# One kernel, one core: row vectors spread by products, weight chunks of 512 columns, and ten slots for gathered rows

## What is computed

```python
def first_block(...):
    for l in range(2):
        sh1, sc1, g1, sh2, sc2, g2 = split(silu(c) @ ada_w[l] + ada_b[l], 6)
        mix = hybrid_mixer(modulate(x, sh1, sc1), ...)
        x = layer_norm(ALPHA * x + (1 + g1) * mix, ln1_g[l], ln1_b[l])
        ffn = peer(modulate(x, sh2, sc2), ...)
        x = layer_norm(ALPHA * x + (1 + g2) * ffn, ln2_g[l], ln2_b[l])

def peer(h, ...):                       # 8 heads x 16 picks = 128 experts for each token
    u = u_tab[experts]                  # rows of 1024 float32
    act = gelu(sum(u * h)) * g
    return sum(act * v_tab[experts])
```

## Time and profile before

| | |
|---|---|
| time, median of 3 runs | 2900.17 us (2894.32 to 2902.61) |
| the profiled execution, its own time | 2893.22 us |
| its span, first to last instruction | 2891.4 us |
| PE, DVE, ACT, POOL busy | 1891.9, 1803.3, 374.6, 1071.4 us |
| mean granted clock of PE | 0.80 of full speed |
| DMA | 860.86 MB, mean 298 GB/s |
| gathers (software queue) / SP's loads | 538.12 MB / 321.24 MB |

### The profile page before, as it was taken

The page is one execution under the profiler, slowest core; times in us unless marked ns, Lnnn a source line. Parts: engine busy times, 40 slices in busy tenths (PEclk is TensorE's granted clock), DMA queues, the critical chain, the costliest instruction groups (busy, mean ns, idle before and its releaser), DMA issues.

```text
span 2891.4 us, 23615 instructions
## 1 busy us (share of the span) xinstructions
PE 1891.9 (65%) x8197; PEld 1332.9 (46%) x8197; DVE 1803.3 (62%) x3281; ACT 374.6 (13%) x830; POOL 1071.4 (37%) x1047
## 2 busy tenths in 40 slices
PE   7889444185644363454364467767188999988998
PEld 4668111064342151142251156643157786477873
DVE  1436999889678889979889986676944200142001
ACT  1311001022102010002011000000014100131000
POOL 1002444577355555755556765465600000000000
PEclk8989556586776685776678788889579999999999
DMA  8366999999999999999999999999860544512443
GB/s 288 111 217 226 399 399 401 369 376 374 371 402 404 400 401 391 336 368 399 399 403 374 339 348 392 368 405 405 323 237 30 189 150 156 189 61 90 157 146 116
DMA packets 359975, 860.86 MB, mean 298 GB/s; under 512 B 23721, under 2 KB 146865, under 8 KB 359729
## 3 DMA queue, kind: packets, MB, share of 16 engines
q0 software_dynamic: 148288, 538.12, 48.4%
q1 hardware_dynamic: 211568, 321.24, 31.9%
HBM read 858.23 MB, written 1.05 MB: 297 GB/s over the span
## 4 chain that ended last, share of the span: by engine, by line
PE 36%; DMA 33%; DVE 14%; issue 11%; POOL 3%; ACT 2%; SPq 0%; DVEq 0%; ACTq 0%
PE bank L927 13%; DMA RING<-in_peer_v,EX 10%; PE bank L415 8%; DMA W<-in_w_ada 6%; PE bank L941 5%; DMA W<-in_ada_w 4%; DMA RING<-in_peer_u,EX 3%; PE bank L424 3%; DMA WORK<-in_peer_u,EX 3%; DMA W<-in_w_up 2%; DVE ACC L1680 2%; POOL RING L1041 2%; PE bank L447 2%; DMA W<-in_w_gate 2%; DMA WORK<-in_peer_v,EX 2%
## 5 line engine op out<-in xcount | busy, mean ns | idle before, releaser
L927 PE MATMUL bank<-HT,W 128*128 128x256 f32 x2112 | 482.0, 392 | 61.6 <-DMA W<-in_w_up 30.3
L927 PEld LDWEIGHTS bank<-HT,W 128*128 128x128 f32 x2112 | 414.8, 197 | 128.6 <-DMA W<-in_w_up 33.9
L1041 POOL DMA_INDIRECT RING<-in_peer_u,EX x343 | 326.4, 952 | 378.8 <-DVE ACC L1662 244.7
L1662 DVE SCALAR_TENSOR_TENSOR ACC<-RING,hrows 128x1024 bf16<-128x1024 f32 x343 | 406.2, 1217 | 79.9 <-DMA RING<-in_peer_u,EX 77.6
L1041 POOL DMA_INDIRECT RING<-in_peer_v,EX x341 | 379.2, 1112 | 206.6 <-DVE hrows L1680 91.5
L447 PE MATMUL bank<-W,CACT 128*32 128x512 f32 x704 | 149.9, 955 | 237.5 <-DMA W<-in_w_ada 135.3
L403 PE MATMUL bank<-consts,XN 128*128 128x128 f32 x208 | 44.6, 397 | 312.4 <-DVE XN L1505 144.6
L415 PE MATMUL bank<-W,HT 128*128 128x256 f32 x992 | 228.7, 394 | 18.6 <-ACT HT L1101 7.4
L941 PE MATMUL bank<-W,WORK 128*128 128x512 f32 x528 | 229.3, 597 | 14.4 <-DVE WORK L2279 14.4
L1041 POOL DMA_INDIRECT WORK<-in_peer_v,EX x171 | 193.7, 1133 | 100.1 <-DVE hrows L1680 39.2
L2279 DVE TENSOR_TENSOR WORK<-WORK,bank 128x256 f32<-128x256 f32 x66 | 27.2, 420 | 321.3 <-ACT WORK L1401 321.3
(11 more groups left out here) (356 smaller groups left out, 2332.1 us busy)
## 6 DMA issues: line engine op xcount, KB each, us to landing
W<-in_w_ada SPq DMA_DIRECT2D x48, 1024.0 KB, 16.4
W<-in_ada_w SPq DMA_DIRECT2D x40, 1024.0 KB, 12.9
W<-in_w_gate SPq DMA_DIRECT2D x33, 1024.0 KB, 5.5
W<-in_w_up SPq DMA_DIRECT2D x33, 1024.0 KB, 5.6
W<-in_w_down SPq DMA_DIRECT2D x33, 1024.0 KB, 5.0
W<-in_w_in SPq DMA_DIRECT2D x32, 1024.0 KB, 13.6
W<-in_peer_wq SPq DMA_DIRECT2D x22, 1024.0 KB, 17.4
W<-in_w_out SPq DMA_DIRECT2D x12, 1024.0 KB, 5.3
```

The source lines that it names most:

```text
L927: mm = pe.matmul(bs[j][:, g * S:(g + 1) * S], w[:, k, j * P:(j + 1) * P], HT[:, k, :], start=(k == 0 and g == 0), stop=(k == DC - 1 and g ...
L1041: gp.indirect_dma_start(SLOT[g % NS], None, rows, bass.IndirectOffsetOnAxis(EX[:, t, k:k + 1], 0))\
L1662: ve.scalar_tensor_tensor(out=JUNK[:, g % 2, :], in0=SLOT[g % NS], scalar=1.0, in1=HB[:, :], op0=ALU.mult, op1=ALU.mult, accum_out=ACTS[:, ...
```

## The change

1. `ROWS` (8 KB of each partition) goes, `ROWM` (4 KB) comes: 20 vectors, one on each of 20 partitions, loaded once by POOL in ten small DMAs. A vector is spread by a product of a column of the identity, broadcast, with `ROWM` (`spread_into`): into a PSUM bank of its own (`spread`, two banks of 512 for a vector), or, for the biases of gates, added in the bank of the gate.
2. The 1 that is added to the gates of the first model comes from ACT's copy (bias `one`), and the DVE instructions that added bias and 1 go.
3. `layer_norm` of layer 0 and the last `scaled_rows` still have rows from loads: the first two by POOL at the start into `HN` and `ACC`, the last two by SP into `HN` and `GA[:, 3, :]`. Of 14 pairs of loaded rows two are left.
4. `NS = 10`; seven slots lie in `RING`.
5. In the feed-forward a chunk is 4 blocks of rows by 512 columns (rows of 2 KB), four banks are open at a time; the last two of 22 columns of blocks stay as they were.
6. The plan of `stage(0, 0, 1)` has eight steps of `c0` in place of nine, since `gate_rows` is one step; ACT no longer waits for `gated` within `ada` of `c0`.

```diff
-        NS = 9
+        NS = 10
-        ROWS = sb("ROWS", [P, 2, D])
+        ROWM = sb("ROWM", [P, D])
+            def spread_into(b, kind, l, hf, start):
+                r = ROW_AT[kind] + l
+                return pe.matmul(b[:, :], ident[0:NROWS, r:r + 1].to_broadcast([NROWS, P]), ROWM[0:NROWS, hf * 512:(hf + 1) * 512],
+                                 start=start, stop=True)
+            def spread(name, kind, l):
+                for hf in range(2):
+                    b = open_bank((*name, hf), "V")
+                    spread_into(b, kind, l, hf, True).then_inc(filled, 1)
...
                         pe.matmul(b[:, :], const("who")[:, who:who + 1].to_broadcast([P, P]), ROWT[:, half, :],
-                                  start=True, stop=True).then_inc(filled, 1)
+                                  start=True, stop=False)
+                        spread_into(b, ("ada_" if p[0] == "b" else "ada2_") + "12"[(q - 8) // 2], int(p[1]), q % 2, False)\
+                            .then_inc(filled, 1)
...
-                load_rows(d["ln1_g"][l], d["ln1_b"][l])
+                spread(("ln1", p, t, 0), "ln1_g", l)
+                spread(("ln1", p, t, 1), "ln1_b", l)
...
                 modulated(p, 2, 2, VA)
+                if who == "l":
+                    spread(("post", "l1", l), ("post_mix", "post_ffn")[l], 1)
-                for c in range(NF // 2):
+                for f0 in range(0, NF, 4):
+                    nf = min(4, NF - f0)
                     bs = []
                     for g, src in enumerate((wg, wu)):
+                        parts = 2 if nf == 4 else 1
+                        for kh in range(parts):
+                            ks = range(kh * DC // parts, (kh + 1) * DC // parts)
+                            w = weight(src[:, ks.start:ks.stop, f0 * P:(f0 + nf) * P])
+                            for j in range(nf):
+                                if g == 0 and kh == 0:
+                                    bs.append(open_bank(("gu", p, f0 + j), "V"))
+                                for k in ks:
+                                    mm = pe.matmul(bs[j][:, g * S:(g + 1) * S], w[:, k - ks.start, j * P:(j + 1) * P], HT[:, k, :], ...)
+                                if g == 1 and kh == parts - 1 and j < nf - 1:
+                                    mm.then_inc(filled, 1)
...
             ada("b1", d["ada_w"][1], [0], FIRST, beside=lambda i: gather(0, 0, 0, 10 * i + 64))
-            load_rows(d["norm_post_mix_2"][0], d["norm_post_ffn_2"][0])
+            spread(("post", "c0", 0), "post_mix", 0)
+            spread(("post", "c0", 1), "post_ffn", 0)
...
             ada("b1", d["ada_w"][1], [0], SECOND)
-            load_rows(d["ln2_g"][0], d["ln2_b"][0])
+            spread(("ln2", "b0", 0, 0), "ln2_g", 0)
+            spread(("ln2", "b0", 0, 1), "ln2_b", 0)
...
+            for name, (src, c0) in {"ada_1": ("ada_b", 2 * D), ...}.items():
+                gp.dma_start(ROWM[ROW_AT[name]:ROW_AT[name] + 2, :], d[src][:, c0:c0 + D]).then_inc(row_vectors, 16)
+            gp.dma_start(HN[:, :], d["ln1_g"][0].partition_broadcast(P)).then_inc(wide_rows, 16)
+            gp.dma_start(ACC[:, :], d["ln1_b"][0].partition_broadcast(P)).then_inc(wide_rows, 16)
...
-            for _ in range(22):
-                next(early)
-            act.wait_ge(mark("gated", "b0"), 1)
             all_of(early)
...
-            def scaled_rows(p, t):
+            def scaled_rows(kind, p, t):
                 inverse(p, t)
+                for i, scalar in enumerate((MV, RSD)):
+                    for hf in range(2):
+                        c = slice(hf * 512, (hf + 1) * 512)
+                        b = wait_full(ve, (kind, p, t, i, hf))
+                        free((kind, p, t, i, hf), ve.scalar_tensor_tensor(
+                            out=X[:, t, c], in0=X[:, t, c], scalar=scalar[:, t, 0:1], in1=b[:, :], ...))
+                    settle()
...
-                for op in (ALU.add, ALU.mult):
-                    rows_here()
-                    for i, gs in enumerate(gates):
-                        for half in range(2):
-                            do(ve.tensor_tensor(GA[:, gs[half], :], GA[:, gs[half], :], ROWS[:, half, :], op), ...)
-                    yield
+                for half in range(2):
+                    for hf in range(2):
+                        c = slice(hf * 512, (hf + 1) * 512)
+                        b = wait_full(ve, ("post", p, half, hf))
+                        for i, gs in enumerate(gates):
+                            ins = ve.tensor_tensor(GA[:, gs[half], c], GA[:, gs[half], c], b[:, :], ALU.mult)
...
-            stage(0, 0, 1, {k: [c0] for k in (0, 3, 5, 10, 16, 20, 22, 26, 30)})
+            stage(0, 0, 1, {k: [c0] for k in (0, 3, 8, 14, 18, 20, 24, 29)})
```

## The result

The kernel after takes 2933.81 us (median of 4 runs, 2928.57 to 2953.69) against 2900.25 us: a ratio of 1.0131, with a 95% interval of 1.0082 to 1.0181. I had forecast 2872 us and a range up to 2904. The slow-down is real: 34, 35 and 43 us by the medians.

What follows compares the result with a forecast made beforehand. DMA and DVE were taken to bound the middle in alternating phases, PE alone the tail. Terms 5.1 - 17 - 4 - 9 - 5.5 - 1.3 - 4 + 7.3 gave -28.4 us, hence 2872 us from the 2900.2 median; range 2842 to 2904.

Steps and rivals of the forecast that it cites:

- Bytes, -17: Middle, 444 to 1494 us: nine pairs of row loads go, 6.5 of them counting, -17 us (-10 to -24).
- DVE's work, -5.5: Middle: shorter `gate_rows` near 545 us, -4.3, and one gate instruction fewer in `stage(0,0,0)`, -1.2; together -5.5 us.
- Order and the first `ln2`, -1.3: Earlier `c0` steps save 5.5 us of a 14.4 us DVE wait; half-by-half feeding of `scaled_rows` loses 4.2; sum -1.3.
- SP's queue, -4: Near 547 us: SP no longer waits for `gate_rows`, so weights of `c0` load in the DMA dip, -4 us (0 to -5.5).
- The tenth slot, -9: Middle, nine DMA dips: one more gather under way or waiting in each, -9 us (0 to -18).
- Chunks of 512 columns, -4: Feed-forward of `c0`: 2 KB rows load faster, -4 us; grouping by four sets bounds of -16 and +10.
- rival B: `c0` feed-forward: groups of four make DVE wait, +35 us if the clock falls below some 0.65; 2911 us; chance 0.12.
- Start, +5.1: Up to 289 us: two wide rows loaded by POOL, +2.6, and two added gate products, +2.5; +5.1 us (+1 to +6).
- End, +7.3: Tail: four added gate products, 5.1 us, and the spread for `gate_row`, 1.1 us twice; +7.3 us (+4 to +8).
- A: Middle set by DVE's order, not DMA, so bytes, queue and chunks bring nothing: 2897 us; chance 0.14.
- C: Middle: slot, order and chunks reach their far ends together, a larger gain: 2848 us; chance 0.09.
- D: DVE returns slots late, so ten are held as nine were, and products cost PE more at the low clock: 2885 us; 0.06.

Runs made afterwards that it cites:

- before_again: The kernel before, unchanged, run for a second profile: 2902.87 us in its single profiled execution.
- plan_back: Kernel after with nine slots, the old 256-column chunks and the eight `c0` steps of `stage(0, 0, 1)` in the rounds of the kernel before: ratio 1.0048.
- before_third: The kernel before, unchanged, run for a third profile, on a chip without slow issue: 2892.79 us.
- early_only_2: Kernel after with old 256-column chunks and gate biases added in bank `mr` ahead of the weights' products: 0.9967 without slow issue; as `early_only`, 0.9999 with it.
- paired: Kernel after with the feed-forward steps of `c0` in `stage(1, 1, 0)` taken two and two: 1.0024 without slow issue, 1.0124 with it.
- c256_again: Kernel after with the old feed-forward chunks (256 columns, two banks open), ten slots kept, run again: ratio 1.0056.
- early_late: Kernel after with old 256-column chunks, gate biases added early in bank `mr`, and POOL's two wide rows loaded later: 2881.03 us, ratio 0.9956.
- bytes_back: Kernel after with nine slots, old 256-column chunks and nine pairs of loads put back that nobody reads: ratio 1.0147.

## Why the prediction was wrong, point by point

**Bytes, -17: right in kind, and near in size.** From gather 288 to 768, where six of the nine pairs fell, the stretch went from 833 us (`before_again`) to 820 (`plan_back`, same chip, nine slots in both); six pairs are 15.7 us. With ten slots it went from 833 (`before_third`) to 818 (`early_only_2`). On the chips with slow issue this gain is taken away again: 834 us in the kernel after.

**DVE's work, -5.5: done, not gained.** DVE is busy 482.4 in place of 489.0 us up to gather 288, -6.6, but the stretch from gather 0 to 288 is 560, 554 and 560 us in the three profiles, in place of 555, 558 and 557, because of the waits of the next point.

**Order and the first `ln2`, -1.3: the failing step is "-5.5" for the wait of 14.4 us.** It fell, to 6.0 us, and the wait for `SD` behind it grew from 5.8 to 18.7 us. In all twenty profiles the sum of the two is 19 to 25 us, so DVE waits for one chain, the weights of `ada` of `b1` through PE and ACT, and what it doesn't wait at one place it waits at the other. The half-by-half feeding cost 4.4 us, as forecast (4.2). The sum of the three went from 20.2, 22.1 and 21.2 us in the profiles of the kernel before to 29.1, 25.3 and 26.9 in those of the kernel after: +6 in place of -1.3.

**SP's queue, -4: no.** The dip near 540 us moved to 550 to 585 us. Slices of 5 us of `early_only_2`, 440 to 640 us:

```profile
GB/s 399 398 395 402 399 399 403 403 399 394 404 402 401 399 400 399 391 399 390 398 392 393 373 331 351 364 201 325 334 395 395 395 386 370 390 397 394 394 394 394
```

Summed below 400 it lost 6.5 us of DMA (373 to 334), against 8.9 in the earlier trace rows: -2.4.

**The tenth slot, -9: of the right sign, size open.** 4 us by the one pair on chip A, whose intervals overlap.

**Chunks of 512 columns, -4: the largest error, +18 to +21, and the step that failed most.** The mechanism of the term is there. In `paired` the chunks of `w_gate` land in 13.6 us in place of 24.4, and the total is 403 GB/s. Queue 1 moved 14.75 MB in 25.9% of 150 us, 380 GB/s while busy, against 342 with rows of 1 KB. The Trainium skill, page "DMA: Bandwidth & Descriptors", section "Specifications", has 512 B as the smallest transfer at line rate; a tenth between 1 and 2 KB speaks against taking that as the whole story. What failed is the sentence "with the grouping by four, which can shorten or lengthen DVE's waits by some 10 us", and behind it rival B's "2 to 8 us of waiting for each of four groups". The cycle was worked out correctly there, and so were PE's 22 us. Two things were missing. DVE comes back after three rounds in two of the four groups only, and after two rounds in the others; without any idle time of PE the four waits would be 8, 6, 12 and 13 us. And PE's slow issue, which no row of before showed, adds 9, 7, 4 and 2 us to them, and stands before the first group as well, where DVE waits 16.1 us. The price of +18 to +21 was measured on chips with slow issue alone (A and C). What the chunks cost without it is open. An estimate: on chip D `paired` is 15 us slower than `early_only_2`, which has neither these chunks nor the gates' products; the latter were 16.5 us on chip C, so nothing is left there for the chunks when the steps are taken in pairs.

**Start, +5.1: right in kind, small in size.** +7.4 to +9.8. The wide rows delay PE's transposes from 42.0 to 46.6 us, 4.6 for 2.6; the gates' products are 3.3 (`c256_again` less `early_only` at gather 0) for 2.5.

**End, +7.3: mis-sized.** The gates' products were priced at 1.27 us each, and what stands behind them at nothing. `c256_again` needs 18.0 us more than before from the last gather on, `early_only` 4.8: 13.2 for my 5.1. In the kernel after it was 12.5, 17.8 and 5.5, and the kernel before itself varies by 8. How low the clock is at the gates goes with it: in the five profiles in which all four products shown above took 2.07 or 2.08 us, this part is 18 to 22 us longer than in the first profile of the kernel before; in the six in which three of them took 1.12 to 1.21 us, it is 5 to 14 us longer. On chip B the difference is 6.9 us (`plan_back` 12.4, `early_late` 5.5), near the forecast. By the times on chip C the gates' products cost 16.5 us in all, start and end, for a forecast of 7.6.

**What no term covered: slow issue.** 9 us (`early_only`) to 29 us (`paired`) between chips.

Laid end to end, against the forecast of -28: chunks 23 (with the slow issue that falls into them), the gates' products 9, wide rows 2, order and `ln2` 7, SP's queue 2, slow issue 9 or more come to some 52 of the 62 us by which I was off. The rest isn't assigned. That the kernel on a chip of the kind of B or D would still be slower than before wasn't measured; `paired` there was, at 1.0024.

Of the rivals, A falls with `bytes_back`, and C with the dips that stayed. Of D, one half came true, the products that cost PE more at the lower clock; the half on the slot is open. B had the side and the cycle right, but not its condition, a clock below 0.65, and its price for the groups, +35, was above the +18 to +21 measured. Its 2911 us were too low all the same, since the gates' products and the slow issue came on top.

Of the signs I had named, 848 MB came out, the start nearly (7 to 10 us for 5), and the clock above 0.7 from 1690 to 1910 us (0.83). The end was 12.5, 17.8 and 5.5 us longer for 7. The slices near 570 us fell to 201 GB/s, the waits for the feed-forward banks were 90 us where I wanted them below 40, and the last gather came 25 to 33 us later. "The waits only change their name" was to be the sign of an error and was one, though much of it is the slow issue's.

## What to carry to other kernels

Two waits of one engine behind the same chain are one wait: taking work away before the first only feeds the second, so price the chain. When several banks are filled by the same last chunk, what counts is the time from the step that frees the bank the producer needs to the consumer's next step: write that time down for each group, since the rounds between steps aren't equal. Taking the steps of a group together may give some of it back (8 us here, not beyond doubt). And compare two kernels on one chip: a difference between chips was as large as the effects looked for. Put a small added product where its engine waits for weights anyway, not behind them, where the clock is low.

## What the runs showed of the hardware

- PE issued single products 0.7 to 2.8 us apart for up to 30 us on some chips, with no wait on record and a granted clock of 0.50 in the longest stretches, and on others it never did, with the same program; a difference of 9 to 29 us. In the longest stretches gathers alone were in the DMA (407 to 410 GB/s), but neither they nor the low clock brought it about: at a granted clock of 0.50 and with gathers alone PE ran without a gap from 916.8 to 926.2 us of the same profile. The cause stays open.
- A product of 512 columns (two records) took 1.12 to 2.08 us behind two waits for weights; the same sum ahead of such a wait took 1.04.
- Weights with rows of 2 KB moved at 380 GB/s while their queue was busy, those with rows of 1 KB at 342, both beside gathers.
- While gathers and weights both had work, the two queues moved the same number of packets, 1782 and 1782 in 25 us, and so 6.47 and 3.55 MB: the one with the longer rows gets more bytes.
- Eight microseconds lay between two profiles of one kernel in its last 790 us, and five at the gathers before.
